# Preparing the second branch's input in pairs of feature tiles, one pair between each two gate products of the first branch

## What is computed

```
z = h @ w_in                      # q_A k_A v_A | q_B k_B v_B i f | o_B | gate_A | gate_B
ya = local_attention(qa, ka, va)
hm, C, n, m = mlstm_chunkwise(qm, km, vm, i_pre, logf, C0, n0, m0)
yb = jax.nn.sigmoid(og) * head_norm(hm, prm['mlstm_norm_w'])
merged = jax.nn.sigmoid(ga) * (ya @ prm['w_proj_a']) + jax.nn.sigmoid(gb) * (yb @ prm['w_proj_b'])
x = layer_norm(ALPHA * x + g1 * (merged @ prm['w_out']), prm['ln1_w'], prm['ln1_b'])
f, conv_new = conv_ffn(h, conv_buf, prm['w_up'], prm['b_up'], prm['conv_w'], prm['conv_b'], prm['w_down'])
```

## Time and profile before

| | |
|---|---|
| median of 3 runs | 1912.1 us (1911.89 to 1915.02) |
| profiled execution | 1912.31 us, of which the span in the profile is 1910.5 us |
| PE busy | 1845.1 us, 97% of the span |
| PE weight loads busy | 1773.8 us |
| DVE busy | 1031.9 us, 54% |
| ACT busy | 595.6 us, 31% |
| POOL busy | 550.7 us, 29% |
| stage of interest | about 828 to 930 us of the span |

### The profile page before, as it was taken

How to read it: one execution, slowest core, us unless ns; L and a number is a source line. 1 busy time by engine, 2 the same in 40 slices (tenths; PEclk the granted TensorE clock), 3 DMA queues, 4 the chain that set the end, 5 groups by cost and what they waited for, 6 DMA issues and landing times.

```text
span 1910.5 us, 28962 instructions
## 1 busy us (share of the span) xinstructions
PE 1845.1 (97%) x11791; PEld 1773.8 (93%) x11791; DVE 1031.9 (54%) x1781; ACT 595.6 (31%) x1287; POOL 550.7 (29%) x310
## 2 busy tenths in 40 slices
PE   7999999998999999998999999999999999999995
PEld 6998778887999999998999999999999999999995
DVE  5825776674433334454344778545536445554587
ACT  2113334533222223243111474222222222222335
POOL 2332211221222222222246345333323323323330
PEclk9999999999999999999999999999999999999998
DMA  9543231112343333256334001111111111111112
GB/s 390 166 139 106 90 112 47 68 50 88 112 131 108 127 107 118 85 176 211 112 135 138 24 12 56 45 51 50 45 45 45 45 52 48 45 45 45 45 38 78
DMA packets 78749, 173.29 MB, mean 91 GB/s; under 512 B 9156, under 2 KB 42308, under 8 KB 78488
## 3 DMA queue, kind: packets, MB, share of 16 engines
q1 hardware_dynamic: 55112, 119.63, 19.3%
q10 hardware_dynamic: 23504, 51.80, 7.7%
HBM read 139.18 MB, written 32.24 MB: 90 GB/s over the span
## 4 chain that ended last, share of the span: by engine, by line
PE 84%; DVE 7%; ACT 3%; DVEq 2%; issue 1%; DMA 1%; ACTq 1%; SPq 0%; POOL 0%; POOLq 0%
PE acc L441 31%; PE px L722 16%; PE acc L722 10%; PE px L732 8%; PE acc L732 5%; PE px L699 2%; ACT probs L866 1%; PE acc L699 1%; DVE stage L1253 1%; DVEq L1255 1%; PE px L612 1%; PE px L610 1%; PE px L611 1%; DMA ada_ring<-in_w_ada 1%; PE px L511 1%
## 5 line engine op out<-in xcount | busy, mean ns | idle before, releaser
L441 PE MATMUL acc<-x_hilo_a,w_hilo 128*128 128x352 f32 x4032 | 681.1, 326 | 7.2 <-DVE x_c L1477 6.5
L441 PEld LDWEIGHTS acc<-x_hilo_a,w_hilo 128*128 128x128 f32 x4032 | 646.4, 189 | 18.9 <-issue 9.3
L406 POOL CAST w_hilo<-w_raw 128x1024 fp32r<-128x1024 f32 x132 | 144.0, 1091 | 1198.6 <-PE acc L441 660.9
L408 POOL TENSOR_TENSOR w_hilo<-w_raw,w_hilo 128x1024 fp32r<-128x1024 f32 x132 | 339.8, 2574 | 10.6
L722 PE MATMUL px<-x_hilo_a,w_hilo 128*128 128x352 f32 x1968 | 317.5, 321 | 0.0
L722 PEld LDWEIGHTS px<-x_hilo_a,w_hilo 128*128 128x128 f32 x1968 | 313.7, 188 | 0.3
L722 PE MATMUL acc<-x_hilo_a,w_hilo 128*128 128x352 f32 x1200 | 194.2, 321 | 0.0
L722 PEld LDWEIGHTS acc<-x_hilo_a,w_hilo 128*128 128x128 f32 x1200 | 191.4, 188 | 0.0
L732 PE MATMUL px<-ffn_act,w_hilo 128*128 128x352 f32 x864 | 146.9, 325 | 0.0
L732 PEld LDWEIGHTS px<-ffn_act,w_hilo 128*128 128x128 f32 x864 | 141.0, 190 | 0.2
L1130 ACT ACTIVATE u_rows<-px,ffn_consts 128x352 f32<-128x352 f32 (+2 forms) x110 | 49.6, 479 | 234.2 <-PE px L722 234.2
(11 more groups left out here) (233 smaller groups left out, 2168.0 us busy)
## 6 DMA issues: line engine op xcount, KB each, us to landing
w_raw<-in_w_panels SPq DMA_DIRECT2D x141, 512.0 KB, 3.6
z_spill<-stage ACTq DMA_DIRECT2D x41, 528.0 KB, 3.0
adaT_ring<-in_w_adaT SPq DMA_DIRECT2D x32, 512.0 KB, 4.0
stage<-z_spill ACTq DMA_DIRECT2D x20, 528.0 KB, 4.9
ada_ring<-in_w_ada SPq DMA_DIRECT2D x16, 512.0 KB, 14.7
zc<-z_spill SPq DMA_DIRECT2D x8, 1024.0 KB, 9.3
x_c<-in_x SPq DMA_DIRECT2D x8, 528.0 KB, 15.5
x_c<-in_x ACTq DMA_DIRECT2D x8, 528.0 KB, 3.8
```

Source lines behind the costliest of these rows:

```text
L406: nc.gpsimd.tensor_copy(to[:, 0, :], raw[:, s, :]).then_inc(w_hi, 1)
L408: nc.gpsimd.tensor_tensor(to[:, 1, :], raw[:, s, :], to[:, 0, :].bitcast(F32), ALU.subtract).then_inc(w_ready, 1)
L441: last = mm(acc[:, n, 0:NW], whl[:, slot, wi, k * P:(k + 1) * P], rhs[:, xi, k, n * NW:(n + 1) * NW], start=(k == 0 and j == 0), stop=(k = ...
```

## The change

A `y` in the order now stands for two feature tiles, m and m+1. Each engine does the two in an interleaved way: both sigmoids, then both copies on ScalarE; both products, then both subtractions on VectorE. Both tiles' loads are issued after the pair. The order places one pair after a1, a2, a3 and a4.

```
-BRANCH_ORDER = ... "a0 a1 g2 y0 g3 a2 g4 y1 a3 g5 y2 y3 a4 g6 y4 y5 a5 g7 y6 y7 a6 a7"
+BRANCH_ORDER = ... "a0 a1 g2 y0 g3 a2 y2 g4 a3 y4 g5 a4 y6 g6 a5 g7 a6 a7"
...
                 else:
-                    act.wait_ge(og_in[m % 2], 16 * (m // 2 + 1))
-                    A(yb_stage(m)[0], yb_stage(m)[0], ACT.Sigmoid).then_inc(sg_rdy, 1)
-                    act.wait_ge(yb_rdy, m + 1)
-                    A(XB[:, 0, m, :], yb_stage(m)[0], ACT.Copy).then_inc(yb_hi, 1)
+                    for i in (m, m + 1):
+                        act.wait_ge(og_in[i % 2], 16 * (i // 2 + 1))
+                        A(yb_stage(i)[0], yb_stage(i)[0], ACT.Sigmoid).then_inc(sg_rdy, 1)
+                    for i in (m, m + 1):
+                        act.wait_ge(yb_rdy, i + 1)
+                        A(XB[:, 0, i, :], yb_stage(i)[0], ACT.Copy).then_inc(yb_hi, 1)
                     if m + 2 < KT:
                         load_yb(m + 2)
+                        load_yb(m + 3)
...
                 elif kind == "y":
-                    og, hn_m = yb_stage(m)
-                    dve.wait_ge(hn_in[m % 2], 16 * (m // 2 + 1))
-                    dve.wait_ge(sg_rdy, m + 1)
-                    V.scalar_tensor_tensor(og, og, small[:, C_NW + m:C_NW + m + 1], hn_m, ALU.mult, ALU.mult).then_inc(yb_rdy, 1)
-                    dve.wait_ge(yb_hi, m + 1)
-                    V.tensor_tensor(XB[:, 1, m, :], og, XB[:, 0, m, :].bitcast(F32), ALU.subtract).then_inc(yb_lo, 1)
+                    for i in (m, m + 1):
+                        og, hn_i = yb_stage(i)
+                        dve.wait_ge(hn_in[i % 2], 16 * (i // 2 + 1))
+                        dve.wait_ge(sg_rdy, i + 1)
+                        V.scalar_tensor_tensor(og, og, small[:, C_NW + i:C_NW + i + 1], hn_i, ALU.mult, ALU.mult).then_inc(yb_rdy, 1)
+                    for i in (m, m + 1):
+                        dve.wait_ge(yb_hi, i + 1)
+                        V.tensor_tensor(XB[:, 1, i, :], yb_stage(i)[0], XB[:, 0, i, :].bitcast(F32), ALU.subtract).then_inc(yb_lo, 1)
```

More of the change, by code:

```diff
@@ L116, in rank @@
     return KT * NT + n * KT + m
-BRANCH_ORDER = tuple((s[0], int(s[1])) for s in "a0 a1 g2 y0 g3 a2 g4 y1 a3 g5 y2 y3 a4 g6 y4 y5 a5 g7 y6 y7 a6 a7".split())
+BRANCH_ORDER = tuple((s[0], int(s[1])) for s in "a0 a1 g2 y0 g3 a2 y2 g4 a3 y4 g5 a4 y6 g6 a5 g7 a6 a7".split())
 def ml_part(c):
```

## The result

| | before | changed |
|---|---|---|
| median of 10 runs each | 1912.38 us (1911.52 to 1916.21) | 1906.53 us (1905.93 to 1909.23) |
| ratio to before, 95% interval | | 0.9965 (0.9956 to 0.9973) |
| profiled execution, its span | 1912.31, 1910.5 | 1906.7, 1904.9 |
| panel 1's last group to panel 7's last group | 77.02 us | 69.99 us |

It runs from the moment VectorE takes the last column group of panel 1 to the same moment of panel 7, six panels of 11.45 us, so **68.70 us** is a stage without any loss. Before it was 930.33 - 853.31. This time leaves out whatever happens ahead of or behind the stage.

The account below looks back on a forecast made before the run. TensorE, busy 97% of the span, bounds the kernel. Of 8.33 us removable, lateness of 0.1, 0.5 and 0.1 left 7.7, less 0.5 for handovers 7.2; 1912.3 - 7.2 = 1905.1 us, range 1903.8 to 1909.5.

Parts of the forecast that it names:

- the likeliest case: Whole kernel: the forecast and full hiding of the pairs counted as one case, 1903.8 to 1907 us, chance 0.76.
- its allowance of 0.5: Stage: 0.5 us taken off the 7.7 us gain for handovers that had been put at nothing, leaving 7.2.
- What is removed, 8.33 us: TensorE, panels 3 to 7: 4.97 and 1.54 us idle, 1.52 of slow clock and 0.3 for two restarts can be won.
- A pair fits into one panel's time: Between gate products: from T, when VectorE can take a panel's last column group, about 11.45 us suffice; panels late by tenths.
- The first product ends 1.1 after GpSimd: VectorE: GpSimd's split holds the shared ports, so a pair's first product ends 1.12 us after its second step, about T + 4.75.
- The 2.91 us from the last subtraction to the end of the gate product's first third: VectorE and ScalarE, behind each pair: the old 2.54 us plus 0.37 for the gate load now queued there.
- Loads landing at E + 7.5: A pair's four loads: the fourth lands 7.5 us after E, the first issue, at 1.3 us per further load.
- The slack of 1.3: Pairs 2,3 and 4,5: transfers may land 1.3 us later before the pairs wait, since GpSimd is later until then.
- The gain stays behind the stage: After the first projection everything follows TensorE at the same distance, so the gain should stay; rival giving it back, chance 0.07.
- Everything hidden: Rival, stage: with a flat surcharge of 1.3 us no panel is late, 8.3 us won, 1904.0; counted within chance 0.76.
- The late transfers: Rival: fourth load lands at E + 10.7, panels 4 and 5 late by 2.0 us; 1908.0 or 1911.0, chance 0.12.
- the slower case: Rival: fourth load lands later than about E + 11.3, gaps and slow clock eat the 8.3 us; 1917.5 at E + 13, chance 0.05.

Follow-up runs that it names:

- Run 1: The kernel before with two serial y between any two gate products from a1 to a5, not interleaved; stage 80.05 us, ratio to before 1.0018.
- run 2: The changed kernel's interleaved pairs placed close to the old places, none between a2 and a3; stage 69.38 us, ratio to before 0.9966.
- Run 4: The changed kernel without GpSimd's split for panels 4 to 7 of the first projection; stage 68.68 us, 1906.44 us in one run.
- run 9: The changed kernel with one more 528 KB transfer between each pair's even and odd tile's loads; stage 72.82 us, 1912.99 us in one run.
- runs 3 and 6: The changed kernel with the next gate sigmoid between the even and odd tile's loads, measured twice; stage 68.68 and 68.70 us, ratios to before 0.9958 and 0.9964.
- run 8: The changed kernel with pair 4,5's last subtraction done three times instead of once; stage 73.95 us, 1908.54 us in one run.
- 7: The changed kernel with three more 528 KB transfers between each pair's even and odd tile's loads; stage 80.88 us, ratio to before 1.0030.

## Why the prediction was right

It gave 1905.1 us with a range of 1903.8 to 1909.5; measured were 1906.5, 1.4 above, inside the likeliest case's own range (to 1907). The mechanism was right. That the size in the stage came out near, 7.0 us won where 7.2 were forecast, is in part luck: a slow issue that nothing in the forecast stands for cost about 1 us, the 0.5 of lateness that it expected at panel 4 did not come, and its allowance of 0.5, meant for handovers, took up the rest. By its steps:

- **What is removed, 8.33 us.** Right: the gaps of 4.97 and 1.54 and the slow clock's 1.52 are gone, and the stage became 7.03 us shorter.
- **A pair fits into one panel's time.** Right, to 0.4 us or better, in two of the three pairs that have a deadline. From T to the end of the next gate product's first third, with the 0.41 of the restart, pair 2,3 took 12.08 us (forecast 12.03) and pair 4,5 11.63 (forecast 12.03), against 11.45. Pair 0,1 took 12.39 where the forecast had 11.55. Run 1 shows that serial y do not fit and run 2 that the pairs' places matter little.
- **The first product ends 1.1 after GpSimd.** Right for pair 2,3: 869.38 + 2.37 = 871.75, GpSimd's step ended at 870.64. In pair 4,5 the first product slipped in between GpSimd's two steps (1.52 us) and the second was held instead, to 885.20, 1.12 after GpSimd's 884.08. That pair ended at T + 8.05, not at the forecast's T + 8.7, since only one product was left behind GpSimd's step. That the whole time and not a flat 1.3 is blocked shows in pair 0,1, where the second product took 3.45. This bears out the Trainium skill (SBUF — State Buffer, section "SBUF: two separate sides"), by which one of the two holds the shared ports for its whole instruction; GpSimd loses too, its step taking 3.30 where it takes 2.40 alone. Run 4 shows the same by taking the split away. (The prediction counts three ends in its rows and they show two; the third, in the same timeline, is 866.92 + 2.58 = 869.50, 1.11 after GpSimd's 868.39.)
- **The 2.91 us from the last subtraction to the end of the gate product's first third.** This term was too small in one place: 3.94 in pair 0,1 (863.61 to 867.55), because of the issue of 1.65; about 3.0 and 3.2 in the next two. So the losses came as 1.1, 0 and 0.2 at panels 3, 4 and 5, where I had 0.1, 0.5 and 0.1. In sum 1.3 against 0.7. (The prediction's 930.33 - 922.7 is 7.6 and not 7.7; this moves its 1905.1 by 0.1.) That panel 4 was not late follows from panel 3 having been: pair 2,3 needed 12.08 from T2, and panel 3, late by 1.1, gave it 12.54.
- **Loads landing at E + 7.5.** Too early by 0.4 to 2: measured 9.5, 7.9 and 8.5. The trace before already hinted at it: of the loads issued at 858.97 and 859.33 the second took 7.1 us, so a second load, beside a weight panel, landed at E + 7.5, where I put the fourth. What VectorE waited for loads cost nothing here. In pair 2,3 the 0.98 passed while GpSimd's step held the product anyway, and the 0.22 lay in the time that panel 3 had lost. In pair 4,5 the 0.62 passed during GpSimd's step, and pair 6,7 has time to spare. The slack of 1.3 was not there in pair 2,3, as run 9 shows.
- **The gain stays behind the stage.** It did in this profile: 979.3 us from panel 7's last group to the end, 980.2 before. But ahead of the stage the changed kernel's profile is 2.3 us later (panel 1's last group at 855.57, before at 853.31), where the program is the same. The windows show where most of it comes from, before first, then changed:

```profile
220.00:240.00 20.00, 18.03 (x123) 15.14 (x122) 14.49 (x31) 7.33 (x26) 3.39 (x2) 1.00 0.31 105
```

```profile
220.00:240.00 20.00, 18.47 (x113) 15.36 (x112) 14.37 (x31) 7.51 (x26) 2.09 (x2) 0.91 0.31 107
```

  An idle spell of 1.5 to 1.6 us among the attention's small matmuls stands in both. Behind it the clock was halved in one execution and not in the other. In all eleven profiles it is the same: where this window shows 1.00 (before, and the runs 1, 3 and 8) panel 1's last group comes at 853.3 to 853.7, where it shows 0.91 (the other seven) at 855.6 to 856.4. So a single pair of profiles is uncertain by 2 us on either side of the stage, and 7.0 won in the stage agree with 5.2 to 8.4 by the interval.
- **The rivals.** *Everything hidden* rested on a flat surcharge, and that is refuted: beside GpSimd a product took 2.37, 2.77 and 3.45 us, and always ended 1.1 after GpSimd. Its result, nothing lost in the stage, is reached in the runs 3 and 6 by another way, the order of ScalarE's queue. The late transfers and the slower case exist in the runs 9 and 7, mixed with the longer queue; this change does not reach them. What 2 us of idle time do to the clock was left open; run 8 answers: at 2.05 it was halved.

## What to carry to other kernels

Two chains that change engine at every step cost little more than one if their steps are interleaved: here, from T, one tile took 7.2 us before (876.20 to 883.37), two in series 13.7, and two interleaved 8.0 to 8.7. Ask of such a group whether it fits between two deadlines of the engine that is the bound, and count from the last step everything that is queued behind it on the other engines, DMA issues too. Here that stretch took 3.0 to 3.9 of the 11.45 us, at least 1.3 of it issues. An instruction that somebody waits for belongs ahead of loads that nobody needs yet: in the stage that won the last 1.3 to 1.5 us (runs 3 and 6), though it did not show in the whole time. An idle spell of the tensor engine can cost more than itself: the one of 2.05 us in run 8 cost 3.75.

## What was not expected of the hardware

- **The clock after short idle spells.** Gaps of 1.49 and 1.54 us in the stage left the granted clock at 1.00, gaps of 2.05, 2.50, 3.21, 3.86, 3.94 and 4.97 were each followed by panels that took 1.5 to 2.5 us longer, and the windows behind them go down to 0.50 to 0.52. Behind the idle spells of 1.27 and 1.71 us with few matmuls between, it was halved in three profiles of eleven, and behind the one of 1.5 to 1.6 among small matmuls in seven of eleven. Each time costs about 2 us, as much as small changes here are worth, and it is the main difference between executions of the same code that I found. Why it falls in one execution and not in the next is not shown.
- **One DMA issue of ScalarE takes 1.0 to 1.7 us instead of 0.45,** 7 to 9 us behind panel 1's last group, in the changed kernel (1.65), its repetition (1.41), and the runs 2 (0.98), 3 (1.31), 6 (1.55), 7 (1.41), 8 (1.53) and 9 (1.44); not before and not in the runs 1 and 4. All eleven profiles have one packet of the queue that fetches instructions near this place. In the eight with a slow issue it moves between 0.6 us ahead of that issue's start and 0.3 us behind it (862.57 to 862.82 in the changed kernel, where the issue starts at 862.76). In the other three it moves while ScalarE's queue issues nothing (862.06 to 862.31 before). So the two go together; that the fetch is the cause was not tried.
